# A two-block transformer kernel: the second tile's input projections, attention and retention moved beside the first tile's expert gathers, and every fourth pick added on VectorE

## What is computed

```
xn = rmsnorm(h, attn_norm);  proj = xn @ w_in              # q_a k_a v_a q_r k_r v_r g_r gate_a gate_r
y_a = sliding_window_attention(q_a, k_a, v_a, sinks) @ w_attn_branch    # window 128
y_r = retention(q_r, k_r, v_r, g_r) @ w_ret_branch         # chunks of 128, a state from chunk to chunk
h = h + (sigmoid(gate_a) * y_a + sigmoid(gate_r) * y_r) @ w_out
hn = rmsnorm(h, ffn_norm);  qry = hn @ w_peer_query        # then: best 16 of 128*128 experts per head, 8 heads
u, vv = expert_down[idx], expert_up[idx]                   # one row of 2048 each, per token, head and pick
h = h + sum_k gates_k * gelu(hn . u_k) * vv_k;  x2 = rmsnorm(h, final_norm)
```

## Time and profile before

| | us |
|---|---|
| median of 3 runs (3369.48 to 3376.61) | 3370.17 |
| the profiled execution, its own time | 3370.57 |
| its span, first to last instruction | 3368.6 |
| mean granted TensorE clock, share of 2.4 GHz | 0.973 |

### The profile page before, as it was taken

How to read it: one execution, slowest core, us unless ns; L and a number is a source line. 1 busy time by engine, 2 the same in 40 slices (tenths; PEclk the granted TensorE clock), 3 DMA queues, 4 the chain that set the end, 5 groups by cost and what they waited for, 6 DMA issues and landing times.

```text
span 3368.6 us, 24788 instructions
## 1 busy us (share of the span) xinstructions
PE 3126.0 (93%) x8509; PEld 1377.8 (41%) x8509; DVE 1086.3 (32%) x1806; ACT 556.1 (17%) x1330; POOL 607.6 (18%) x598
## 2 busy tenths in 40 slices
PE   8999999998999999898698898898899989999999
PEld 4444444443434344343244333343344533333344
DVE  1030010015434335335564644543332132222220
ACT  1110010011111111112133321221222110001010
POOL 0000000002332233233343333333300000000000
PEclk9999999999999999999999999999999989999999
DMA  7524448869999999999999999999967749999982
GB/s 247 166 101 150 150 171 284 314 241 368 421 421 421 422 421 422 421 421 417 418 408 419 403 419 419 419 419 418 417 238 271 265 179 415 422 422 422 422 314 75
DMA packets 249572, 1143.92 MB, mean 340 GB/s; under 512 B 14416, under 2 KB 17024, under 8 KB 146304
## 3 DMA queue, kind: packets, MB, share of 16 engines
q1 hardware_dynamic: 175120, 605.17, 46.2%
q0 software_dynamic: 74352, 537.48, 38.6%
HBM read 1140.49 MB, written 2.10 MB: 339 GB/s over the span
## 4 chain that ended last, share of the span: by engine, by line
PE 60%; DMA 29%; issue 3%; DVE 3%; ACT 2%; DVEq 1%; SPq 0%; POOL 0%; ACTq 0%; POOLq 0%
DMA W<-in_peer_expert_down,big 16%; PE bank L843 13%; PE bank L834 12%; PE bank L1316 12%; DMA W<-in_w_expert_up 7%; PE bank L912 7%; PE bank L1413 4%; PE bank L1468 3%; PE bank L1192 2%; DMA XS<-in_peer_expert_up,big 2%; DMA XT<-in_peer_expert_up,big 2%; DVE W L2252 1%; DMA W<-in_peer_expert_up,big 1%; PE bank L1397 1%; PE bank L1383 1%
## 5 line engine op out<-in xcount | busy, mean ns | idle before, releaser
L2252 DVE CUSTOM_DVE_ANT_0 W<-W,big 128x2048 f32<-128x2048 f32 x256 | 586.3, 2291 | 842.9 <-DMA W<-in_peer_expert_down,big 842.3
L1316 PE MATMUL bank<-XS,big 128*128 128x512 f32 x1040 | 500.6, 629 | 87.8 <-DMA XS<-in_peer_expert_up,big 46.0
L771 POOL DMA_INDIRECT W<-in_peer_expert_down,big x256 | 264.5, 1033 | 1386.8 <-issue 684.9
L834 PE MATMUL bank<-W,XT 128*128 128x512 f32 x960 | 417.6, 595 | 4.8 <-issue 4.8
L1316 PEld LDWEIGHTS bank<-XS,big 128*128 128x128 f32 x1040 | 204.3, 201 | 366.4 <-issue 279.9
L843 PE MATMUL bank<-W,XT 128*128 128x512 f32 x704 | 308.4, 596 | 0.0
L1316 PE MATMUL bank<-W,big 128*128 128x512 f32 x520 | 252.5, 631 | 58.3 <-ACT big L1705 36.6
L834 PEld LDWEIGHTS bank<-W,XT 128*128 128x128 f32 x960 | 182.5, 191 | 227.3 <-issue 226.8
L1316 PE MATMUL bank<-XT,big 128*128 128x512 f32 x488 | 229.4, 614 | 31.6 <-ACT big L1705 16.5
L1700 ACT ACTIVATE small<-small 128x1 f32<-128x1 f32 x256 | 51.8, 202 | 1190.5 <-DVE small L2252 1175.6
L1413 PE MATMUL bank<-W,XS 128*64 128x512 f32 x1024 | 226.7, 596 | 14.2 <-DMA W<-in_w_expert_up 11.6
(11 more groups left out here) (337 smaller groups left out, 2319.5 us busy)
## 6 DMA issues: line engine op xcount, KB each, us to landing
W<-in_w_in SPq DMA_DIRECT2D x102, 2048.0 KB, 8.4
W<-in_w_expert_gate SPq DMA_DIRECT2D x68, 1024.0 KB, 15.0
W<-in_w_expert_up SPq DMA_DIRECT2D x68, 1024.0 KB, 17.0
W<-in_w_out SPq DMA_DIRECT2D x32, 2048.0 KB, 11.9
big<-in_w_expert_down SPq DMA_DIRECT2D x32, 2048.0 KB, 12.6
W<-in_w_ret_branch SPq DMA_DIRECT2D x16, 2048.0 KB, 11.7
W<-in_w_peer_query SPq DMA_DIRECT2D x16, 2048.0 KB, 13.6
W<-in_w_attn_branch SPq DMA_DIRECT2D x8, 2048.0 KB, 10.8
```

Source lines behind the costliest of these rows:

```text
L771: pool.indirect_dma_start(down_row(n), None, down_t, row).then_inc(down_in[n % DOWN_ROWS], 16)
L834: mm = pe.matmul(ps[t][:, :], lhs(k0 + k, t), w[:, k, :], start=first and k == 0, stop=last_unit and k == kn - 1)
L1316: mm = pe.matmul(bank[4 * (n // P) + c][:, :], DIAG[:, n % 4, :], up_row(n)[:, c * CH:(c + 1) * CH], start=n % P == 0, stop=n % P == P - 1)
L2252: dve.tensor_tensor_reduce(out=down_row(n), in0=down_row(n), in1=HN[n // P], scale=1.0, scalar=0.0, op0=ALU.mult, op1=ALU.add, accum_out=d ...
```

## The change

Tile 1's part of the first stage leaves the first stage. There each unit now meets tile 0 alone (8 matmuls, `unit_in`), with the small work of tile 0; only tile 1's input transposes stay (step `x1`). The 30 units are read from HBM a second time in tile 0's ticks 10 to 44 (`in1`, 28 of them as 4 blocks of 1024 columns, 2 of 8 blocks of 512), with tile 1's RoPE, attention (groups are renumbered: 0 and 1 are tile 0's, 2 and 3 tile 1's) and retention at ticks 14 to 53. The keys, values and state of tile 0 that tile 1 needs are kept in `KV0` and `STATE`. The 44 wide units move to ticks 54 to 104 at one per 1.1 ticks. At start x is loaded tile by tile, and the small loads of gains and rows wait until two units are used. Picks with n % 4 == 3 get no diagonal and no matmul: VectorE adds weight times up row to `H` itself (`add_weighed`), after the next pick's dot.

Cut to its core:

```diff
+    order += [("in1", 1, g, j) for g in range(8) for j in range(2 if g == 1 else 4)]
...
+IN1 = [(QA, 1024), (KA, 512), (QR, 1024), (KR, 1024), (VR, 1024), (VR + 1024, 1024), (GR, 1024), (GR + 1024, 1024)]
...
+BY_DVE = [n for n in range(PICKS) if n % 4 == 3]
+BY_PE = [n for n in range(PICKS) if n % 4 != 3]
...
+    for i, key in enumerate([key for key in ORDER if key[:2] == ("in1", 1)]):
+        when[key] = at + i if i < 6 else int(at + 6 + (i - 6) * 1.25)
+        put(pe, when[key], *key)
...
-            when[key] = int(at + i * 2.15)
+            when[key] = int(at + i * 1.1)
...
             for half in range(2):
-                sp.dma_start(H[:, :, half * 1024:(half + 1) * 1024], x[:, :, half * 1024:(half + 1) * 1024]).then_inc(x_loaded[half], 16)
+                sp.dma_start(H[:, 0, half * 1024:(half + 1) * 1024], x[:, 0, half * 1024:(half + 1) * 1024]).then_inc(x_loaded[half], 16)
             load(0)
             load(1)
             sp.dma_start(C[:, P:], consts[:, P:CONST_W]).then_inc(c_loaded, 16)
...
+            sp.dma_start(H[:, 1, :], x[:, 1, :]).then_inc(x_loaded[2], 16)
...
+            pool.wait_ge(w_used, 2)
...
-                if earlier is not None:
-                    pool.wait_ge(added, earlier + 1)
+                if earlier in BY_DVE:
+                    pool.wait_ge(added_dve, DVE_COUNT[earlier] + 1)
+                elif earlier is not None:
+                    pool.wait_ge(added, PE_COUNT[earlier] + 1)
...
+                for k in range(8):
+                    if q == 0 and k % 4 == 0:
+                        pe.wait_ge(xt_act if k else xt_dve, half + 1)
+                    mm = pe.matmul(bank[q % 4][:, :], xt(8 * half + k, 0), slot(u)[:, k, :],
+                                   start=half == 0 and k == 0, stop=half == 1 and k == 7)
                 mm.then_inc(w_used, 1)
...
+            def in1_unit(g, j):
+
+                at, width = IN1[g]
+                ks = 4096 // width
+                i = INDEX["in1", 1, g, j]
+                pe.wait_ge(w_loaded[SLOT[i]], LANDED[i])
+                for c in range(width // CH):
+                    if j == 0 and g == 0:
+                        pe.wait_ge(query_kept, 3 + c)
+                    elif j == 0:
+                        pe.wait_ge(set_free, IN1_SETS[g - 1] + c + 1 if g != 2 or c == 0 else IN1_SETS[1])
+                    for k in range(ks):
+                        mm = pe.matmul(bank[4 + c][:, :], xt(ks * j + k, 1), slot(i, width)[:, k, c * CH:(c + 1) * CH],
+                                       start=j == 0 and k == 0, stop=ks * j + k == KC - 1)
+                mm.then_inc(w_used, 1)
...
+                if n in BY_PE:
+                    m = PE_COUNT[n]
                     b, _, count = UP_ROWS[n]
                     pe.wait_ge(up_in[b], 16 * count)
-                    pe.wait_ge(diag_ready, n + 1)
+                    pe.wait_ge(diag_ready, m + 1)
...
+                    if n in BY_DVE:
+                        weigh_it.then_inc(weight_ready, 1)
+                    else:
+                        act.drain()
+                        act.activation(DIAG[:, m % 4, :], ident, ACT.Copy, scale=wts[:, j:j + 1]).then_inc(diag_ready, 1)
...
+            def add_weighed(n):
+
+                b, _, count = UP_ROWS[n]
+                h, j = H[:, n // P, :], n % TOPK
+                dve.wait_ge(weight_ready, DVE_COUNT[n] + 1)
+                dve.wait_ge(up_in[b], 16 * count)
+                dve.drain()
+                STT(h, up_row(n), wts[:, j:j + 1], h, ALU.mult, ALU.add).then_inc(added_dve, 1)
...
                     dve.tensor_tensor_reduce(out=down_row(n), in0=down_row(n), in1=HN[n // P], scale=1.0, scalar=0.0,
                                              op0=ALU.mult, op1=ALU.add,
                                              accum_out=dots[:, n % BATCH:n % BATCH + 1]).then_inc(dotted, 1)
+                    if n - 1 in BY_DVE:
+                        add_weighed(n - 1)
```

More of the change, by code:

```diff
@@ L55, in order_of_units @@
     return order + [("ple", j) for j in range(8)]
+IN1 = [(QA, 1024), (KA, 512), (QR, 1024), (KR, 1024), (VR, 1024), (VR + 1024, 1024), (GR, 1024), (GR + 1024, 1024)]
+SETS = 15
+IN1_SETS = [SETS + sum(width // CH for _, width in IN1[:g]) for g in range(9)]
+TURNS = 11
 WIDE = ("gate_a", "gate_r", "att", "ret", "mix", "query")
@@ L87 @@
 UP_ROWS = rows_of_up()
+BY_DVE = [n for n in range(PICKS) if n % 4 == 3]
+BY_PE = [n for n in range(PICKS) if n % 4 != 3]
+PE_COUNT = [sum(m < n for m in BY_PE) for n in range(PICKS + 1)]
+DVE_COUNT = [sum(m < n for m in BY_DVE) for n in range(PICKS + 1)]
 CONST_AT = {}
@@ new lines, in turn_in1 @@
+            def turn_in1(m, src, b):
+                if m < 2:
+                    pe.wait_ge(qt_kept, 4)
+                    pe.wait_ge(s_kept, 4)
+                    pe.wait_ge(roped, 5)
+                elif m == 2:
+                    pe.wait_ge(turn_kept, TURNS + 1)
+                    pe.wait_ge(roped, 6)
+                elif m < 5:
+                    pe.wait_ge(probs_kept, m)
+                    pe.wait_ge(roped, 7)
+                else:
+                    pe.wait_ge(attn_kept, 4)
+                    pe.wait_ge(turn_kept, TURNS + 5)
+                    pe.wait_ge(roped, 8)
+                for c in range(2 if m == 2 else 4):
+                    last = pe.transpose(bank[b][:, c * P:(c + 1) * P], P1[:, 1, src + c * P:src + (c + 1) * P], ident)
+                last.then_inc(turned, 1)
@@ new lines, in inner @@
+            def inner(r):
+                if r == 0:
+                    pe.wait_ge(turn_kept, TURNS + 7)
+                else:
+                    pe.wait_ge(ret_stats, HEADS + 1 + 2)
+                    pe.wait_ge(ret_kept, HEADS + 1)
+                for j in range(4):
+                    h = 4 * r + j
+                    mm = pe.matmul(bank[6 + r][:, j * P:(j + 1) * P], P1[:, 1, KR + h * P:KR + (h + 1) * P],
+                                   P1[:, 1, QR + h * P:QR + (h + 1) * P], start=True, stop=True)
+                mm.then_inc(ret_inner, 1)
@@ L1147, in _ @@
             pe.wait_ge(ret_ready, 1)
-            for j in range(4):
-                turn(P1, GR + 512 * j, 512)
+            turn(GR, D)
             branch(0)
@@ L1321, in _ @@
                         wide_unit(kind, what[1])
+                    elif kind == "in1":
+                        in1_unit(*what[1:])
+                    elif kind == "turn_in1":
+                        turn_in1(*what)
+                    elif kind == "inner":
+                        inner(*what)
+                    elif kind == "cross":
+                        cross(*what)
+                    elif kind == "turn_ret":
+                        turn_ret(*what)
                     elif kind == "turn_merged":
@@ L1650, in _ @@
                     keep_gate(n, which)
-            for j in range(4):
-                keep_turned(P1, QR + 512 * j, 512)
+            keep_turned(QR, D)
             for n in range(2, 4):
```

603 lines of the change are left out of this document (393 added, 210 removed).

## The result

| | median, us | ratio to before, 95% |
|---|---|---|
| before (4 runs beside it) | 3369.8 | |
| after (4 runs) | 3340.8 | 0.9909 [0.9882, 0.9936] |
| after, measured again later beside other kernels | 3342.2 | 0.9909 [0.9894, 0.9924] |

The change gains 29 us. The forecast was 3292, a gain of 78. The profiled execution took 3332.3 us, the fastest of its four (up to 3347.4); its span is 3330.5.

The account below looks back on a forecast made before the run. PE bounds the kernel before 784 us, transfers bound the picks (784 to 2460 us). 3370.6 - 240 (first stage) + 149.4 (bytes) + 12 (transfers not full) = 3292 us, range 3268 to 3348.

Parts of the forecast that it names:

- First stage: Before the picks, PE-bound: tile 1's units and small work leave and the start comes earlier, 240 us less.
- Bytes: Tile 0's picks: 30 units read again, 62.9 MB at 421 GB/s, cost 149.4 us.
- The adds save nothing by themselves: Among the picks: VectorE's 64 adds alone gain nothing, since PE isn't the bound there.
- they cost nothing: VectorE's adds fit among the picks: no cost taken, with up to 10 us where VectorE is full.
- What isn't full: Tile 0's picks: small dependent steps keep transfers below full pace, 12 us; 0 to 40 us possible.
- PE and DMA at 97% of each other: Ticks 10 to 104: PE 817 us against transfers' 842 after, 673 against 692 before, so transfers stay full.
- Rival C: Transfers at 404 GB/s in tile 0's picks (+28), first-stage waits (+10): 3315 to 3345 us, 27%.
- Rival B: Two weight slots pace tile 0's ticks, landings of 18.5 us: 106 us more, 3386 us, 8%.
- the argument against B: A late unit holds back picks, gathers pause and weights get the whole bandwidth; no separate size.
- D: Among the picks, VectorE's adds block POOL's descriptors and starve gathers: 150 us more, 3442 us, 2%.
- PE's clock falls where it idles: Among the picks: PE's clock 0.94 to 0.97 against 1.00 before them, making PE later still.

Follow-up runs that it names:

- e3: Kernel before, with only VectorE's 64 adds put in: 3373 us, ratio 1.0006.
- e11: As e6, but all adds on TensorE, none on VectorE: 3312 us, ratio 0.9826; again 3311, 0.9822.
- e6: Changed kernel with VectorE's and ScalarE's steps one to three ticks later where no result is waited for: 3321 us, ratio 0.9848; again 3322, 0.9854.
- e10: As e6, but the 30 input units load the same 2 MB from 2048-column rows (wrong weights): 3307 us, ratio 0.9810.
- e12: e6, e10 and e11 in one, so later steps, long weight rows, all adds on TensorE: 3306 us, ratio 0.9808.
- e5: Changed kernel with every second matmul of tile 1's 30 input units left out: 3316 us, ratio 0.9839.
- e7: As e6, with every second matmul of tile 1's input units left out: 3309 us, ratio 0.9818.

## Why the prediction was right and wrong

**First stage: right.** 241 us left ahead of the first pick (TensorE's first add came at 784.0 us, now at 542.9), 240 forecast; the first unit starts at 13.2, its units take 211 us, and TensorE stays the bound with the transfers at 311 GB/s.

**Bytes: right as a term.** 149.4 us of the 204 by which the picks grew in the profiled execution.

**The adds save nothing by themselves: right (e3); that they cost nothing: wrong**, by 9 us. The working had them buy 65 us of TensorE: it held 907 us of TensorE's work in ticks 10 to 104 against 842 of transfers. The price was too high, since a pick costs 3.60 us where TensorE doesn't wait, not 3.76, and TensorE may lag by the four up rows and catch up in the ticks with picks alone. In e11 ticks 10 to 110 take 903 and 905 us with all adds on TensorE, less than the 917 and 922 of e6; TensorE is busy 885 us of the 903, where the working's prices give 926.

**"What isn't full": the step that failed.** It was priced at 12 us for all of tile 0's picks, from the pace of tile 1's picks. Ticks 54 to 110 alone took 516 us (522 in the second measurement) where bytes want 498, and ticks 10 to 54 took 414 where they want 369: 63 us together, not 12. In before the same ticks, with other work, took 723 where their bytes want 717. TensorE's own work was forecast well (817 us for ticks 10 to 104, 835 measured up to tick 110), what hangs on it was not. The nearest row was no likeness: in tile 0's ticks 10 to 110 of before, VectorE waited 16 us for TensorE in all and never over 3.1 us at once; after the change it waited 203 us, up to 29.2 at once (below, in both kernels, the step in which VectorE adds a mix unit's result to `H`). What the working knew (PE and DMA at 97% of each other) it used as proof that the transfers stay full. But TensorE then runs further behind: when a dot starts, the last add that it has finished is 2 to 5 picks back, in before 1 to 3. So nine times a step written one tick behind TensorE's became a wait in front of the next dot. That cost 20 us (e6), the adds 9 (e11), the short rows 14 alone and 6 on top of these (e10, e12); 3306 is what is left, 14 above the forecast. In that rest, ticks 10 to 54 still take 392 us at a DMA share of 0.99 and 396 GB/s, with TensorE busy 382: full transfers that move less than 421 GB/s are part of it, a TensorE near its end and rings of three and four rows may be others. No run divides it, and why full transfers move less here than in the same ticks of before (421 at 1.01) is open beyond the row length.

```profile
DVE H L2006 <- PE bank L912: 6.1, 4, 3.1
```

```profile
DVE H L2285 <- PE bank L995: 25.8, 4, 22.7
```

**Rival C** named the band (3315 to 3345) in which the time fell and "PE later still", but with transfers at 404 and waits of the first stage, not these waits: it holds the time by its width, not by its mechanism. **Rival B**'s 106 us didn't come: the landing was 14.4 us, not 18.5, and it rose to 18.5 when TensorE's matmuls were halved (e5), which fits the argument against B that gathers pause when TensorE is late. B in small is not excluded. At 14.4 us its own formula gives (14.4 + 6.96)/2 = 10.7 us a unit, 390 for ticks 10 to 54, 21 above the bytes, and TensorE did wait 38 us for these weights. No run gave the loads a third slot. The row length on which B rested did cost 6 to 14 us. **D** is there in small: a down gather of POOL beside a dot takes 2.19 us (824.82, beside the dot at 823.91 in the timeline above) and 0.94 without (793.38); 150 us of cost it was not, since all the adds together cost 9.

## What to carry to other kernels

When two streams are brought within a few per cent of each other, don't stop at comparing their sums: look at which engine will then run behind, and put every step that waits for it as many places later as it lags, except where it waits for the answer itself. In an order written by hand such a wait stands in front of everything behind it, here the dot that keeps the gathers going. A bandwidth read in one mix of transfers is not a price for another: 421 GB/s in before was 401 in e7, both with full engines. And moving work off an engine that isn't the bound gained nothing in any pair of kernels here, and cost 9 us even where the engine was otherwise busy 96 to 99% of the time.

## What was not expected of the hardware

Transfers at full share moved 400 GB/s with 4 KB and 2 KB weight rows beside the gathers and 406 with 8 KB rows (600 to 800 us of e6 and e10). And where VectorE took a quarter of the adds and TensorE idled more, its granted clock was lower: 0.90 in tile 1's picks of after, 0.95 in before; 0.97 in ticks 54 to 110 of e6, 1.00 in e11. So part of the slack that the adds made was given back as slower matmuls: some 640 records of tile 1's wide units took 593 to 595 ns each in e11 and 609 to 618 in after. Idle time alone doesn't set it, though, as the prediction's "PE's clock falls where it idles" has it: from 1600 to 1680 us of before PE is busy 55 of 80 us at a clock of 1.00.
